# The front of a one-core block kernel: modulation columns by channel tile, fewer parameter loads ahead, sums by transposes

## What is computed

```python
c_act = jax.nn.silu(c)                                  # c: 1 x 1024
mod = c_act @ w_mod + b_mod                             # 6 x 1024 columns
sh1, sc1, g1, sh2, sc2, g2 = jnp.split(mod, 6, axis=-1)
h = rms_norm(x) * (1.0 + sc1) + sh1                     # 512 x 1024
proj = h @ w_in                                         # 1024 x 10272
```

## Time and profile before

| | |
|---|---|
| median of 3 runs | 1370.19 us (1369.15 to 1370.76) |
| the profiled execution | 1371.04 us, its span 1369.7 us |
| PE busy | 1355.0 us, 99% |
| DVE, ACT, POOL busy | 66%, 46%, 18% |

### The profile page before, as it was taken

The page is one execution under the profiler, slowest core; times in us unless marked ns, Lnnn a source line. Parts: engine busy times, 40 slices in busy tenths (PEclk is TensorE's granted clock), DMA queues, the critical chain, the costliest instruction groups (busy, mean ns, idle before and its releaser), DMA issues.

```text
span 1369.7 us, 24508 instructions
## 1 busy us (share of the span) xinstructions
PE 1355.0 (99%) x9502; PEld 1094.8 (80%) x9502; DVE 900.6 (66%) x1274; ACT 628.7 (46%) x1000; POOL 241.3 (18%) x254
## 2 busy tenths in 40 slices
PE   8999999999999999999999999999999999999998
PEld 5788888888887888878888888888888877777776
DVE  4687877887648867775568542334444687877865
ACT  4566555665554522332245432123433465555533
POOL 0000000000028789760022500000000000000220
PEclk9999999999999999999999999999999999999999
DMA  9445444444455676553333333333333232213221
GB/s 342 138 137 141 119 119 131 126 121 123 146 142 150 164 203 202 151 173 92 96 90 93 108 93 108 92 93 93 106 94 92 74 105 68 83 56 93 64 73 77
DMA packets 276009, 163.46 MB, mean 119 GB/s; under 512 B 6573, under 2 KB 264242, under 8 KB 275898
## 3 DMA queue, kind: packets, MB, share of 16 engines
q1 hardware_dynamic: 269530, 158.90, 39.8%
q10 hardware_dynamic: 6368, 3.00, 0.8%
HBM read 159.59 MB, written 2.29 MB: 118 GB/s over the span
## 4 chain that ended last, share of the span: by engine, by line
PE 88%; DVE 4%; issue 2%; POOL 2%; ACT 2%; DMA 1%; ACTq 0%; SPq 0%; DVEq 0%; POOLq 0%
PE PS L742 23%; PE PS L744 22%; PE PS L743 22%; PE PS L942 1%; POOL mbuf L607 1%; PE PS L1019 1%; PE PS L1021 1%; PE PS L1020 1%; PE PS L1354 1%; PE PS L963 1%; PE PS L1356 1%; PE PS L1355 1%; PE PS L1257 1%; PE PS L1268 1%; POOL mbuf L602 1%
## 5 line engine op out<-in xcount | busy, mean ns | idle before, releaser
L742 PE MATMUL PS<-Hh,whi 128*128 128x512 f32 x1096 | 443.1, 404 | 1.0 <-DVE wlo L2115 0.5
L744 PE MATMUL PS<-Hh,wlo 128*128 128x512 f32 x1096 | 427.8, 390 | 0.0
L743 PE MATMUL PS<-Hl,whi 128*128 128x512 f32 x1096 | 427.2, 390 | 0.0
L2115 DVE TENSOR_TENSOR wlo<-raw,whi 128x1024 fp32r<-128x1024 f32 (+2 forms) x211 | 275.0, 1304 | 116.9 <-ACT whi L1457 116.3
L1457 ACT ACTIVATE whi<-raw 128x1024 fp32r<-128x1024 f32 (+2 forms) x215 | 222.6, 1036 | 169.5 <-PE PS L744 119.3
L742 PEld LDWEIGHTS PS<-Hh,whi 128*128 128x128 f32 x1096 | 205.8, 188 | 50.0 <-issue 6.2
L744 PEld LDWEIGHTS PS<-Hh,wlo 128*128 128x128 f32 x1096 | 205.7, 188 | 44.2
L743 PEld LDWEIGHTS PS<-Hl,whi 128*128 128x128 f32 x1096 | 206.1, 188 | 39.9 <-issue 0.7
L602 POOL TENSOR_TENSOR mbuf<-mbuf,cact 128x1024 f32<-128x1024 f32 x32 | 66.0, 2061 | 409.0 <-DMA mbuf<-in_w_mod_dram 402.9
L607 POOL TENSOR_TENSOR mbuf<-mbuf 128x512 f32<-128x512 f32 x68 | 102.4, 1505 | 5.3
L742 PE MATMUL PS<-YBh,whi 128*128 128x512 f32 x256 | 99.6, 389 | 0.0
(11 more groups left out here) (484 smaller groups left out, 1964.6 us busy)
## 6 DMA issues: line engine op xcount, KB each, us to landing
raw<-in_w_in_dram SPq DMA_DIRECT2D x106, 512.0 KB, 3.9
raw<-in_w_ff_dram SPq DMA_DIRECT2D x64, 512.0 KB, 3.7
mbuf<-in_w_mod_dram SPq DMA_DIRECT2D x32, 512.0 KB, 4.2
crow<-cum_rows SPq DMA_DIRECT2D x32, 256.0 KB, 4.5
raw<-in_w_branch_ssm_dram SPq DMA_DIRECT2D x16, 512.0 KB, 3.6
wm<-in_w_mod_dram SPq DMA_DIRECT2D x6, 1024.0 KB, 9.6
erow<-exp_rows SPq DMA_DIRECT2D x24, 256.0 KB, 5.0
raw<-in_w_out_dram SPq DMA_DIRECT2D x9, 512.0 KB, 3.6
```

Source lines behind the costliest of these rows:

```text
L742: pe.matmul(bank[:, :], whi[s][:, k, :], xh[:, kk, :], start=kk == 0, stop=False)
L743: pe.matmul(bank[:, :], whi[s][:, k, :], xl[:, kk, :], start=False, stop=False)
L744: last = pe.matmul(bank[:, :], wlo[s][:, k, :], xh[:, kk, :], start=False, stop=t == end - 1 and k == (order or range(kt))[-1])
L2115: v.tensor_tensor(wlo[s][:, 0:kt, :], raw[s][:, 0:kt, :], whi[s][:, 0:kt, :].bitcast(F32), ALU.subtract).then_inc(s_wlo, 1)
```

## The change

Pieces of w_mod: for each channel tile m two loads of 128 columns (512 KB, rows of 512 bytes), scale first, then shift, both into wm[m]; the first three weight tiles follow the first three channel tiles. One row product per channel tile (8 of 256 columns in place of 10), one copy of it, and two transposes that take the four partial rows as they are to PSUM columns; DVE adds the four columns by a reduction and waits for its result before the two column operations. The pieces' semaphores thus reach 32 instead of 16, and the later counts on them change by 16.

ACT's queue loads only c and b_mod; the other five vectors go behind the last piece of w_mod on SP's queue, with the ten of before, and are turned in a transpose of their own, which DVE copies out in pieces. ACT runs a silu on a constant before c is there. PE's order is new throughout: four fillers instead of ten ahead of x, the first row product behind the spread of the root, the transpose of the bias and the last copies of x, and the last parts one channel tile at a time. POOL no longer makes selc and filler. The fillers now wait for POOL's sixth constant and write bank 2.

```diff
-        for p, piece in enumerate(MOD_ROWS):
-            load_mod0(*piece)
-            if p in (1, 3, 5):
-                load((1, 3, 5).index(p))
-
-        sp.wait_ge(s_wm[3], 16)
-        for to, ap in fill2:
+        for m in range(KT):
+            load_mod0(m)
+            if m < 3:
+                load(m)
+
+        sp.wait_ge(s_wm[7], 32)
+        sp.wait_ge(s_par2, N_BMOD)
+        for to, ap in fill1[2:] + fill2:
             sp.dma_start(to, ap).then_inc(s_par2, 16)
...
         def x_turned(c):
...
-                    pe.wait_ge(s_pc, 3)
+                    pe.wait_ge(s_cact, 1)
...
-        keep_busy(4, 0)
         pe.wait_ge(s_par, 16)
         pe.transpose(BK[5][:, 0:8], pr[1][0:8, :], ident[0:8, 0:8]).then_inc(s_pt, 1)
-        keep_busy(6, 0)
-        x_turned(0)
-        x_turned(1)
...
+        keep_busy(4, 0)
+        for c in range(NC):
+            x_turned(c)
...
+        def mod_sums(m):
+            pe.wait_ge(s_mrow, m + 1)
+            if m > 0:
+                pe.wait_ge(s_modc, 2 * m)
+            for j in range(2):
+                ms = pe.transpose(BK[6][:, j * 128:j * 128 + 128], mrow[m % 2][:, j * 128:j * 128 + 128], ident[:, :])
             ms.then_inc(s_ms, 1)
 
-        pe.wait_ge(s_const, 13)
         pe.wait_ge(s_xt0, 4)
-        mod_rows(0)
         pe.wait_ge(s_xrs, 1)
...
+        pe.wait_ge(s_xt1, 2)
+        pe.wait_ge(s_par2, N_BMOD)
+        pe.transpose(BK[5][:, 128:184], pr[1][0:56, :], ident[0:56, 0:56]).then_inc(s_pt, 1)
+        pe.wait_ge(s_xt0, 6)
+        keep_busy_half(4)
+        mod_rows(0)
+        keep_busy_half(3)
+        mod_sums(0)
+        keep_busy_half(5)
         mod_rows(1)
-        pe.wait_ge(s_xt1, 2)
-        keep_busy(2, 5)
-        mod_sums(0)
+        part(0, 0)
         mod_sums(1)
-        keep_busy_half(6)
+        keep_busy_half(9)
         mod_rows(2)
-        keep_busy_half(3)
-        mod_rows(3)
-        pe.wait_ge(s_xt0, 6)
-        part(0, 0)
-        mod_sums(2)
-        mod_sums(3)
-        keep_busy_half(9)
         part(1, 0)
         part(0, 1)
+        mod_sums(2)
         part(1, 1)
+        part(2, 0)
+        mod_rows(3)
+        part(2, 1)
+        mod_sums(3)
+        part(0, 2)
+        part(1, 2)
         mod_rows(4)
+        part(2, 2)
+        mod_sums(4)
...
+        part(0, 6)
+        part(1, 6)
+        part(2, 6)
         pe.wait_ge(s_par2, N_PAR2)
...
         for t in range(3):
-            part(t, 6, 7)
+            part(t, 7)
...
         act.dma_start(*fill1[0]).then_inc(s_par, 16)
-        act.wait_ge(s_par, 16)
-        for to, ap in fill1[1:]:
-            act.dma_start(to, ap).then_inc(s_par, 16)
+        act.dma_start(*fill1[1]).then_inc(s_par2, 16)
+        act.wait_ge(s_pc, 1)
+        act.activation(small[:, 63:64], EPS, ACTF.Silu)
         act.wait_ge(s_pt, 1)
...
+        for m in range(KT):
+            mod_row(m)
+            if m < 3:
+                hi(m)
+            h_hi(m)
...
+        for b in range(4):
             x_copy(b, 0)
         v.wait_ge(s_rx, 5)
         v.reciprocal(small[:, 4:8], small[:, 4:8]).then_inc(s_xrs, 1)
+        x_copy(0, 1)
         x_copy(2, 1)
...
+        def h_cols(m):
+            total = small[:, 32:34]
+            v.wait_ge(s_ms, m + 1)
+            own(v.tensor_reduce(total, BK[6][:, 0:256].rearrange("p (b g r) -> p b g r", g=4, r=32)[:, :, :, 0],
+                                mybir.AxisListType.X, ALU.add))
+            v.wait_ge(s_dve, nown)
...
-        for m in range(2):
+        for m in range(KT):
             h_cols(m)
             h_scaled(m)
-            lo(m)
+            if m < 3:
+                lo(m)
             h_lo(m)
```

More of the change, by code:

```diff
@@ L261, in build_program @@
     X_BANKS = (3, 4, 6, 7), (0, 1, 2, 5)
-    MOD_ROWS = [(i, at, 128) for at in (0, 128) for i in (4, 0)] + [(j + i, 0, 256) for j in range(1, 4) for i in (4, 0)]
-    of_cols = lambda m: m if m < 2 else m // 2 + 1
     x_half = lambda b, half: XT[:, 2 * b:2 * b + 2, 256 * half:256 * half + 256]
@@ L580, in pool_program @@
         pool.tensor_copy(identb[:, :], ident[:, :]).then_inc(s_const, 1)
-        for i in range(2):
-            pool.tensor_tensor(selc[:, i:i + 1], ident[:, 64 * i:64 * i + 1], ident[:, 64 * i + 32:64 * i + 33],
-                               ALU.add).then_inc(s_const, 1)
-        pool.wait_ge(s_const, 7)
-        pool.tensor_tensor(selc[:, 0:1], selc[:, 0:1], selc[:, 1:2], ALU.add).then_inc(s_const, 1)
+        pool.wait_ge(s_const, 4)
         pool.tensor_copy(triub[:, :], triu[:, :]).then_inc(s_const, 1)
-        for i in range(4):
-            pool.tensor_copy(filler[:, i * 128:(i + 1) * 128], ident[:, :]).then_inc(s_const, 1)
         own = 0
@@ L780, in keep_busy, with keep_busy_half @@
                           start=True, stop=True)
-        def keep_busy_rounded(n, width, bank=5):
-            for i in range(n):
-                pe.matmul(BK[bank][:, 0:width], filler[:, i % 2 * 128:i % 2 * 128 + 128], filler[:, 0:width],
-                          start=True, stop=True)
-        def keep_busy_half(n, bank=5):
+        def keep_busy_half(n, bank=2):
+            pe.wait_ge(s_const, 6)
             for i in range(n):
@@ L913, in dt_steps @@
                 if s == 19:
-                    pe.wait_ge(s_modc, 10)
+                    pe.wait_ge(s_modc, 16)
                     pe.wait_ge(s_hb, 8)
@@ L2137, in x_copy @@
             v.tensor_copy(x_half(b, half), x_bank(b, half)).then_inc(s_xt0, 1)
-        for b in range(2):
+        for b in range(4):
             x_copy(b, 0)
-        v.wait_ge(s_pt, 2)
-        cols_of(BK[5][:, 128:256], pcB, 128, 1.0)
-        for b in range(2, 4):
-            x_copy(b, 0)
-        x_copy(0, 1)
         v.wait_ge(s_rx, 5)
         v.reciprocal(small[:, 4:8], small[:, 4:8]).then_inc(s_xrs, 1)
+        x_copy(0, 1)
         x_copy(2, 1)
-        def h_cols(i):
-            m, n = (i, 1) if i < 2 else (2 * i - 2, 2)
-            at = m if i < 2 else 2 * m
-            v.wait_ge(s_ms, 2 * i + 2)
-            v.scalar_tensor_tensor(out=opc[:, m:m + n], in0=BK[6][:, at:at + n], scalar=1.0,
-                                   in1=colr("b_mod", 8 + m, n), op0=ALU.add, op1=ALU.add).then_inc(s_modc, 1)
-            v.tensor_tensor(modc[:, m:m + n], BK[6][:, at + 2:at + 2 + n], colr("b_mod", m, n),
-                            ALU.add).then_inc(s_modc, 1)
+        v.wait_ge(s_pt, 2)
+        cols_of(BK[5][:, 128:184], pcB, 56, 1.0)
+        def h_cols(m):
[4 more added lines that the diff above has]
+            v.wait_ge(s_dve, nown)
+            v.scalar_tensor_tensor(out=opc[:, m:m + 1], in0=total[:, 1:2], scalar=1.0, in1=col("b_mod", 8 + m),
+                                   op0=ALU.add, op1=ALU.add).then_inc(s_modc, 1)
+            v.tensor_tensor(modc[:, m:m + 1], total[:, 0:1], col("b_mod", m), ALU.add).then_inc(s_modc, 1)
         def h_scaled(m):
-            v.wait_ge(s_modc, 2 * of_cols(m) + 1)
+            v.wait_ge(s_modc, 2 * m + 1)
             if m == 0:
@@ L2178, in dve_program @@
         v.wait_ge(s_xt0, 6)
-        for m in range(2):
+        for m in range(KT):
             h_cols(m)
             h_scaled(m)
-            lo(m)
+            if m < 3:
+                lo(m)
             h_lo(m)
-        lo(2)
-        for j in range(1, 4):
-            h_cols(j + 1)
-            h_scaled(2 * j)
-            h_scaled(2 * j + 1)
-            h_lo(2 * j)
-            h_lo(2 * j + 1)
-        v.wait_ge(s_pt, 3)
+        v.wait_ge(s_pt, 4)
         cols_of(BK[3][:, 0:128], pcA, 128, 0.5)
-        v.wait_ge(s_pt, 4)
+        v.wait_ge(s_pt, 5)
         cols_of(BK[4][:, 0:rC], pcC, rC, 1.0)
-        v.tensor_scalar(colr("conv_b", 0, 32), colr("conv_b", 0, 32), 0.5, None, ALU.mult).then_inc(s_pc, 1)
-        v.tensor_scalar(colr("ssm_norm_w", 0, 16), colr("ssm_norm_w", 0, 16), 0.5, None, ALU.mult).then_inc(s_pc, 1)
+        late = lambda name, n: BK[3][:, 128 + where[name][1]:128 + where[name][1] + n]
+        own(v.tensor_copy(colr("gm_norm_w", 0, 8), late("gm_norm_w", 8)))
+        own(v.tensor_copy(pcB[:, 112:128], late("final_norm_w", 16)))
+        v.tensor_scalar(colr("conv_b", 0, 32), late("conv_b", 32), 0.5, None, ALU.mult).then_inc(s_pc, 1)
+        v.tensor_scalar(colr("ssm_norm_w", 0, 16), late("ssm_norm_w", 16), 0.5, None, ALU.mult).then_inc(s_pc, 1)
+        v.wait_ge(s_pc, 7)
         c4 = lambda ap: ap.rearrange("p (c h) -> p c h", c=NC)
```

111 lines of the change are left out of this document (36 added, 75 removed).

## The result

The changed kernel takes **1379.66 us** (median of 4 runs, 1378.42 to 1381.42) against 1370.05 for the kernel before in the same measurement: a ratio of 1.0069, 95% interval 1.0057 to 1.0081, so +9.6 us where +3.2 was forecast. It is slower, and above the range given. The profiled execution has a span of 1378.6 us, 8.9 more than before.

A forecast was written before the change was run, and what follows sets the result against it. PE, busy 99% of the span, was taken as the bound: +1.4 us at the end of its parts, +2.4 in all at the first full tile, another +0.8 for broadcasts, sum +3.2, giving 1373.4 us; range 1370.6 to 1377.0.

The forecast's parts named there:

- SP's queue: Parameters issued by 43.4, fourth weight tile landed at some 47.3; both covered by 2.7 us, else up to 1.8 each.
- spread of the root: At the start, the spread on PE comes at 11.1 instead of 13.1, x's fourth piece landing at 9.3.
- PE waiting for the parameter loads: Sign that the prediction is wrong: SP's cover of 2.7 us is gone; no chance of its own.
- the low half of the third weight tile: DVE makes it only behind the third scaled tile; PE stands some 2 us, until 27.85.
- the reduction: On DVE ahead of the two column operations, with a wait for its own result: taken as 0.25 us, between 0.1 and 0.6.
- the low weight tile: In a channel tile's chain, usable by PE 3.15 us after the sum's start in the new order.
- the short tail: Only six products follow the first tile's last; first full tile starts 1.5 us behind PE's end instead of 0.47.
- The +0.8 for the broadcasts: Three broadcasts wait on DVE's parameter columns, 3.4 us later; beyond the 2.4 at the first full tile, another 0.8.
- A, the low clock at the start: Rival: PE at 1.2 GHz when row products start, 3.0 us more, 1376.4; chance 0.28.
- B, less late: Rival: broadcasts have slack, reduction and handovers cost less; +1.0 to +2.4, 1371.2 to 1372.6; chance 0.22.
- C, faster: Rival: from 21.3 PE waits for neither the third low half nor chains; 1368.5 to 1369.5; chance 0.05.

The follow-up runs named there:

- experiment 3: Kernel before with each of its six pieces of 256 columns loaded as two of 128 (512-byte rows): 1371.32 us, ratio 1.0005.
- experiment 5: Changed kernel on the old addresses, by an unused tensor of 8 bytes per partition where selc was: 1372.28 us, ratio 1.0014.
- experiment 9: Changed kernel at the old addresses, last two channel tiles done in one go per weight tile behind the parameter transposes: 1372.47 us, ratio 1.0016.
- experiments 6 to 8: Kernel before with an unused tensor of 32, 64 or 256 bytes ahead of the first weight buffer: 1372.77, 1373.17 and 1370.28 us.
- experiment 11: Changed kernel, old addresses, 15 late loads issued earlier by ACT, their transposes and columns earlier, last two channel tiles in one go: 1370.92 us, ratio 1.0003.
- 10: Changed kernel at its own addresses, with fillers ahead of the parameter transposes and behind the last parts: 1378.95 us, ratio 1.0063.
- 12: Changed kernel at its own addresses, with parameters brought forward and last two channel tiles in one go as in experiment 11: 1376.03 us, ratio 1.0041.
- 2: Changed kernel without SP's wait for the last column piece ahead of the 15 parameter loads: 1374.27 us, ratio 1.0031.
- 4: Changed kernel with channel tiles 2 to 7 loaded in pieces of 256 columns (1024-byte rows): 1376.66 us, ratio 1.0047.

## Why the prediction was wrong

| us from the start | forecast | changed kernel | at the old addresses |
|---|---|---|---|
| spread of the root | 11.1 | 10.42 | 10.16 |
| first row product | 13.4 | 12.47 | 12.21 |
| first sum | 15.1 | 14.13 | 13.88 |
| first part | 19.05 | 18.64 | 17.48 |
| third row product | 22.2 | 23.13 | 20.92 |
| third sum | 24.7 | 25.63 | 23.42 |
| first part of the third weight tile | 27.85 | 28.45 | 26.21 |
| last piece landed, parameters begin | at most 38.1 | 43.86 | 38.17 |
| fourth weight tile issued | 43.4 | 49.49 | 44.14 |
| first full tile | 52.85 | 57.01 | 51.26 |
| time against before | +3.2 | +9.6 | +2.1 |

**The step that failed is SP's queue**: "The last column piece landed by 37.6 before ... if 512-byte rows add at most 0.5, the parameters are issued by 43.4 ... Both are covered by 2.7 us; without that cover they would cost up to 1.8 each." Two things are wrong in it. The first is the rate. The landing time of the last piece was taken over from the kernel before, with an allowance for narrower rows. At the old addresses it comes out: the parameters begin at 38.17 where 38.1 was the bound, though in the kernel before narrower rows alone cost 2.3 (experiment 3). What the prediction lacked is the address. That the diff moves the buffers by 32 bytes, and that this makes the same rows 16% slower, no step of it asked: of `selc` it said only that POOL loses some small operations, for whom nobody waits. The second is the bound on the cost: 1.8 each. The wait for the last piece, fifteen issues and the fourth tile are one chain, so a piece that lands 5.8 later than the 38.1 assumed puts the fourth tile's issue 6.1 later than forecast (49.49 and 43.4), and a cover of 2.7 is gone at once. The same rate also holds up row products, for which the prediction had no wait: the second stands 2.04 and the third 1.37, where at the old addresses they stand 0.94 and 0.35. The list of what would show the prediction wrong did have this case, PE waiting for the parameter loads; it was given no chance, and no price beyond that 1.8 each, and that is where the range was too narrow.

**What held.** The chain of PE's events at the old addresses is the forecast's, each 0.9 to 1.6 sooner (SP's two come 0.1 and 0.7 later): the spread came sooner (x's fourth piece had landed by 8.33, where ACT squares it in experiment 5, and not at 9.3), and the rest kept its distances. PE stands for the low half of the third weight tile, 1.72 us at 26.21 and 1.74 at 28.45, where some 2 were forecast; the reduction is cheap. DVE's timeline of the changed kernel, first and third channel tile:

```profile
14.66 0.17 DVE L2121 TENSOR_REDUCE small<-PS 128x2 f32<-128x8 f32 x1 [3.06 <-PE PS L812]
14.86 0.16 DVE L2124 SCALAR_TENSOR_TENSOR opc<-small,pcB 128x1 f32<-128x1 f32 x1
...
27.12 1.22 DVE L2085 TENSOR_TENSOR wlo<-raw,whi 128x1024 fp32r<-128x1024 f32 x1
```

From the reduction to the operation behind it are 0.20 (14.66 to 14.86), the term taken as 0.25 by the small copy of the earlier trace rows; the low weight tile starts 1.49 behind the sum at 25.63 and PE starts at 28.45, 2.82 instead of 3.15. The first full tile waits for ACT's copy 1.24 in experiment 5, as the short tail was said to make it. The forecast +3.2 stands against +2.1 at the old addresses (interval 0.5 to 3.2), and bringing parameters and tail forward takes back 1.2 to 1.5 of it. The +0.8 for the broadcasts came out smaller: at the old addresses the kernel is 0.8 behind at the first full tile and 1.0 at the triangle product, so 0.2 for them, and PE has no stand there as it has in experiment 9; in the changed kernel what DVE waits for last, until 59.94, is PE and not the broadcasts. That +2.1 lies near +3.2 is therefore in part luck. The events explain 1.0 of the 2.1; the rest, like the last 0.8 of the changed kernel, lies behind the front and is not traced.

**The rivals.** A, the low clock at the start: refuted. The four fillers behind the spread are 0.22 apart in the changed kernel (11.51, 11.73, 11.95, 12.16), so PE was at 2.4 GHz, with four fillers and the rest transposes ahead of them. x's transposes up to 6.4 us last 421 ns at the median, those behind 273. The Trainium skill ("TensorE: Matmul & The Clock Gate", Part 4) says that transpose mode doesn't count as busy in the same way and that the full clock doesn't engage for it; here the clock rose among transposes and stayed up through the rest of them. Four fillers stood ahead of them, so the trace doesn't show that transposes alone would have raised it. The clock did cost time, but later, behind stands of PE. B, less late, is near to what the order costs at the old addresses; C, faster, fell with the stand of PE ahead of 28.45.

## What to carry to other kernels

Compare buffer addresses before and after whenever a diff adds or removes a tensor, however small: here 8 bytes nobody seemed to need held every buffer that the front's weights and pieces land in on a multiple of 256, and their loss was three quarters of the slowdown. Where a queue has a wait for a landing in it with further issues behind, price the whole chain to its last consumer at a lower transfer rate, not only each load's own cover. And when a new order looks bad, put it back on the old addresses before judging it.

## What the hardware showed that I had not expected

- **Starts of rows in SBUF.** Rows of 512 bytes that start 32 or 64 bytes off a multiple of 256 were written at 290 to 293 GB/s instead of 347, rows of 1024 bytes at 346 or 347 instead of 386; a shift by 256 changed nothing (experiments 6 to 8). By time per row that is about 20% and 11% more; counted per row it is the same for both, 0.3 ns, an estimate from these rates (512 bytes at 347 and 290 GB/s take 1.48 and 1.77 ns, 1024 bytes at 386 and 347 take 2.65 and 2.95). So a fixed price for each row fits better than a lower rate. The Trainium skill ("DMA: Bandwidth & Descriptors", How a descriptor splits into AXI transactions) says that a descriptor off a multiple of 256 bytes fetches from the boundary below and pays for the unused bytes. The direction agrees with the runs, and the 256 as far as they go (128 wasn't tried); by its count the 512-byte row would take 17 beats of 32 bytes for a start 32 off, and 18 for one 64 off, instead of 16, so by that estimate 6% or 12% more and not the same 20% for both. What in the engine makes it so is open.
- **The clock behind a stand.** The lower level came behind some stands of PE and not behind others like them. At the old addresses PE stood 1.72 us ahead of 26.21 in experiment 5, 1.71 ahead of 26.24 in experiment 9 and 1.73 ahead of 26.16 in experiment 11, behind the same work. The granted clock of the stretches that follow (the column before the DMA share), first 5, then 11 (two stretches of 2 us each):

```profile
27.00:29.00 2.00, 2.00 (x18) 0.92 (x18) 0.00 (x0) 0.38 (x1) 0.00 (x0) 0.66 1.05 307
29.00:31.00 2.00, 2.00 (x7) 1.57 (x6) 0.40 (x4) 0.00 (x0) 0.00 (x0) 0.50 1.10 328
```

```profile
27.00:29.00 2.00, 2.00 (x23) 1.21 (x22) 0.00 (x0) 0.38 (x1) 0.00 (x0) 1.00 1.14 338
29.00:31.00 2.00, 2.00 (x20) 1.29 (x21) 1.11 (x4) 0.58 (x1) 0.00 (x0) 1.00 1.12 338
```

In 5 it falls to 0.50, and from the fourth to the fifth row product 5.07 us pass (27.07 to 32.14); in 11 (and in 9) it stays at 1.00, and 3.50 pass (27.02 to 30.52). Of the eight profiles of the changed kernel and its variants, which all have this stand (1.71 to 1.94 us), three show a fall behind it (experiments 5, 10 and 12, stands of 1.72, 1.94 and 1.75) and five don't (the changed kernel, 2, 4, 9 and 11). In 5 the loss is hidden by the late weight tiles: in 9, without a fall, the first full tile starts at 51.19 as against 51.26. Each fall costs some 1.5 us where PE's work is on the path. A single profile of a kernel with such stands can therefore be 1.5 us off its neighbour's without any cause in the code. The runs of experiment 5 do spread over 4 us, and the mean granted clock goes with it: 1.000 in the fastest (1370.96), 0.997 in the slowest (1375.01). What decides whether the clock falls I haven't found out.
